# Six input tiles by column halves in place of four: the two gate tiles of the first block join them

## The chip, the cores and the metric

One core of one Trainium2 chip runs the whole program. The metric is device time in microseconds, the median of several executions, in float32 throughout.

## The reference, cut to what matters

Two blocks of two layers each act on 1024 tokens of width 1024 (the first block carries 256 context tokens beside them). Only the first block is touched here. Each of its layers normalizes and modulates the tokens, multiplies by `w_in` (2592 columns), mixes in three branches (a gated depthwise convolution, windowed attention, a gated linear recurrence), and multiplies by `w_out`. The convolution branch:

```python
hl = _rms_norm(xl) * (1.0 + scale[:, None]) + shift[:, None]
pl = _project(hl, w_in)          # a_val, a_glu, a_gate (256 columns each), b_q, b_k, ...

def _conv_branch(p, conv_w, conv_b, ln_w, ln_b):
    u = p['a_val'] * jax.nn.sigmoid(p['a_glu'])
    u = lax.conv_general_dilated(
        u, conv_w[:, None, :].astype(u.dtype), window_strides=(1,),
        padding=((CONV_KERNEL // 2, CONV_KERNEL // 2),),      # CONV_KERNEL = 31
        dimension_numbers=('NWC', 'WIO', 'NWC'), feature_group_count=CONV_WIDTH) + conv_b
    uf = u.astype(F32)
    mu = jnp.mean(uf, axis=-1, keepdims=True)
    var = jnp.mean(jnp.square(uf - mu), axis=-1, keepdims=True)
    u = ((uf - mu) * lax.rsqrt(var + NORM_EPS) * ln_w + ln_b).astype(p['a_val'].dtype)
    return jax.nn.silu(u) * jax.nn.silu(p['a_gate'])
```

The first layer computes the context tokens' branches too, the second only those that the other tokens need.

## The kernel before, in words

Activations lie transposed, channels on the partitions and tokens along the free dimension: 1280 columns in layer 0 (1024 tokens and 256 of context), 1024 in layer 1 for this branch. One *tile* of a projection is 128 output channels: a weight matrix of 1024 x 128, read as eight pieces of 128 x 128. To hold float32 accuracy every operand is split into a rounded part and a remainder (`hi`, `lo`), and each piece takes three matmuls (lines 562 to 564, or 590 to 592: weights hi by h hi, hi by lo, lo by hi). So 512 columns of a tile are 24 matmuls of 128x512.

`stream()` writes the order of all tiles by hand into `SEQ`. SyncE loads the weights in that order into two buffers of `raw` (L434), GpSimd splits them (`split_weights`, L2117 and L2118) once TensorE is through with the tile that used the buffer before (two tiles back in the stream), and TensorE multiplies. The first `SKEW1` tiles of a layer of the first block (glu0, val0, glu1, val1; then come gate0, gate1, bk, bv, q0 ...) are run by column halves: first all of them on columns 0 to 511 (pass 0), then all of them on the rest (pass 1: 512 + 256 columns in layer 0, 512 in layer 1). Their weights are loaded and split once for each pass. The other tiles take all their columns at once. glu0 is run piece by piece as h comes (`project_as_ready`, `row_tile`), with the waits for its accumulators ahead of its first piece.

Each chunk of up to 512 columns takes an accumulator bank, three in turn (`psum_of`: q % 3, `acc_free0` to `acc_free2`), and TensorE may start a chunk only when the one three before it has been read out:

- ScalarE (`sigmoids`, L1115) reads glu0 and glu1 and writes their sigmoid. glu1's waits until VectorE has used up glu0's (`u_ready`).
- VectorE (`gated`, L1657) reads val0 and val1 and multiplies by the sigmoid into `cv_u`.
- ScalarE (L1136) reads gate0 and gate1 and writes their Silu into `x`.

In between, both engines make h for pass 1: VectorE scales a tile (`scaled`, L1582), ScalarE rounds it (`round_h`, L1080), VectorE takes the remainder (`split_h`, L1595), eight times. VectorE's order is four tiles of h, val0's product, four tiles of h, val1's product, then pass 1's products, and then the convolution (L1673 and L1675, 31 taps for each of two channel tiles, `conv_ready` after each). In layer 0 TensorE computes 16 pieces of modulation (L598) after gate1. In both layers it then multiplies bk and waits for the convolution, to average it (L654) and its squares (L659). Behind that come ScalarE's square root by Ln and Exp, its Silu (L1156), VectorE's product with the gate (L1696), and only then may ScalarE read out bk (L1104) and the attention begin.

SyncE stores layer 0's output `x` to DRAM before layer 1 (L498, `store0`), and ScalarE waits for that before it writes a gate into `x`.

Of the kernel before, what the change touches and what calls it, by code (L numbers as in the profile page):

```python
# [16 lines left out]
ACT = mybir.ActivationFunctionType  # L17
# [34 lines left out]

PASS_ALL = [CH_ALL[:1], CH_ALL[1:]]
PASS_LAT = [CH_LAT[:1], CH_LAT[1:]]
SKEW1, SKEW2, SKEWF = 4, 8, 4

ORDER2 = [range(8), (0, 1, 4, 5, 2, 3, 6, 7)]

# [1 line left out]
def stream():  # L60

    seq = []
    for l in range(2):
        every = lambda n: PASS_ALL if l == 0 or n in KV1 else PASS_LAT
        for p in range(2):
            for i, n in enumerate(IN1[:SKEW1]):
                seq.append(("in1", l, i, 8, every(n)[p], p))
        for i, n in list(enumerate(IN1))[SKEW1:]:
            seq.append(("in1", l, i, 8, sum(every(n), []), 0))
        for p in range(2):  # L70
            for d in range(DT):
                seq.append(("out1", l, d, 8, (PASS_ALL if l == 0 else PASS_LAT)[p], p))
    for l in range(2):
        for p in range(2):
            for i in ORDER2[p]:
                seq.append(("in2", l, i, 8, PASS_LAT[p], p))
        for i in range(SKEW2, len(IN2)):
            seq.append(("in2", l, i, 8, CH_LAT, 0))
        for p in range(2):
            for d in range(DT):  # L80
                seq.append(("out2", l, d, 8, PASS_LAT[p], p))
        for p in range(2):
            for i in range(SKEWF):
                seq.append(("up", l, i, 8, PASS_LAT[p], p))
        for f in range(NF):
            if f >= SKEWF // 2:
                seq.append(("up", l, 2 * f, 8, CH_LAT, 0))
                seq.append(("up", l, 2 * f + 1, 8, CH_LAT, 0))
            if f in AFTER:
                g = AFTER[f]  # L90
                last = g == len(GROUPS) - 1
                for p in range(2 if last else 1):
                    for d in range(DT):
                        seq.append(("down", l, (g, d), GROUPS[g][1] - GROUPS[g][0], PASS_LAT[p] if last else CH_LAT, p))
    return seq


SEQ = stream()
INDEX = {e[:3] + e[5:]: g for g, e in enumerate(SEQ)}
FIRST_CHUNK = np.cumsum([0] + [len(e[4]) for e in SEQ]).tolist()  # L100
# [76 lines left out]
def two_mixers(nc, xT, cT, w_mod, w_in1, w_out1, vec1, vec2, vec3, sinks, gla_up,  # L177
# [27 lines left out]
    x = x_[:, :].rearrange("p (j t) -> p j t", t=T)  # L205
# [42 lines left out]
    def norm_buffers(n, p):  # L248

        if n < 2:  # L250
            v = [nt[:, i * W1:(i + 1) * W1] for i in range(5)]
            return v[0], v[1], v[2], v[3:5]
        v = [nt[:, i * W2:(i + 1) * W2] for i in range(7)]
        return v[2 * p], v[2 * p + 1], v[4], v[5:7]
# [93 lines left out]
    sem = {n: nc.alloc_semaphore(n) for n in names}  # L348
# [3 lines left out]
    def columns(n, p):  # L352

        return (0, 512) if p == 0 else (512, 768 if n < 2 else 512)
# [48 lines left out]
    def proj_index(l, name, p=0):  # L403
        return INDEX[("in1", l, IN1.index(name), p)]

    def in2_index(l, name, p=0):
        return INDEX[("in2", l, IN2.index(name), p)]
# [6 lines left out]
    def psum_of(q):  # L414
        return psum[q % 3]


    with block:
        @block.sync
        def _(sp):  # L420
            loaded = [0]

            def load_weights(g):
                kind, l, i, nk, _, _ = SEQ[g]
                if g >= 2:
                    sp.wait_ge(sem["w_split"], g - 1)
                src = {"in1": w_in1, "out1": w_out1, "in2": w_in2, "out2": w_out2, "up": w_ffn}.get(kind)
                if kind == "down":
                    grp, d = i
                    f0, f1 = GROUPS[grp]  # L430
                    src = w_down[l, d, :, f0 * P:f1 * P]
                else:
                    src = src[l, i]
                sp.dma_start(raw[:, (g % 2) * 1024:(g % 2) * 1024 + nk * P], src)\  # L434
                  .then_inc(sem[f"raw_in{g % 2}"], 16)
# [108 lines left out]
        def _(pe):  # L544
# [3 lines left out]
            def row_tile(g, kt, hi, lo, ready, before):  # L548

                _, _, _, nk, chunks, _ = SEQ[g]  # L550
                wh, wl = w_hi[:, (g % 2) * 1024:], w_lo[:, (g % 2) * 1024:]
                if kt == 0:
                    pe.wait_ge(sem["w_split"], g + 1)
                    for ci in range(len(chunks)):
                        q = FIRST_CHUNK[g] + ci
                        if q >= 3:
                            pe.wait_ge(sem[f"acc_free{q % 3}"], q // 3)
                ws = slice(kt * P, (kt + 1) * P)
                pe.wait_ge(sem[ready], before + kt + 1)
                for ci, (t0, n) in enumerate(chunks):  # L560
                    o = psum_of(FIRST_CHUNK[g] + ci)[:, 0:n]
                    mm(o, wh[:, ws], hi[:, kt, t0:t0 + n], start=kt == 0, stop=False)  # L562
                    mm(o, wh[:, ws], lo[:, kt, t0:t0 + n], start=False, stop=False)
                    last = mm(o, wl[:, ws], hi[:, kt, t0:t0 + n], start=False, stop=kt == nk - 1)  # L564
                    if kt == nk - 1:
                        last.then_inc(sem["acc_ready"], 1)
# [465 lines left out]
        def _(act):  # L1032
            A = nc.scalar.activation
            steps = [0]

            def link(ins):

                steps[0] += 1
                ins.then_inc(sem["act_step"], 1)
                act.wait_ge(sem["act_step"], steps[0])  # L1040
# [29 lines left out]
            def round_h(n, p, j):  # L1070

                _, _, _, ts = norm_buffers(n, p)
                t0, w = columns(n, p)
                act.wait_ge(sem[f"t_ready{p}"], 8 * n + j + 1)
                if n >= 2:
                    A(h2_hi[:, j, t0:t0 + w], ts[j % 2][:, 0:w], ACT.Copy).then_inc(sem["hhi_ready"], 1)
                    return
                for c0, cw, r in [(t0, 512, 0), (S, C, 1)][:1 + p]:
                    c = 48 * n + 2 * j + r
                    last = A(h_hi[:, j, c0:c0 + cw], ts[j % 2][:, c0 - t0:c0 - t0 + cw], ACT.Identity, bias=mod[:, c:c + 1])  # L1080
                last.then_inc(sem["hhi_ready"], 1)
# [14 lines left out]
            for l in layers:  # L1096
# [10 lines left out]
                def sigmoids(j, p):  # L1107

                    if j:
                        act.wait_ge(sem["u_ready"], 4 * l + 1 + 2 * p)  # L1110
                    g = proj_index(l, f"glu{j}", p)
                    for ci, (t0, w) in enumerate(SEQ[g][4]):
                        q = FIRST_CHUNK[g] + ci
                        act.wait_ge(sem["acc_ready"], q + 1)
                        link(A(cv_sig[:, t0:t0 + w], psum_of(q)[:, 0:w], ACT.Sigmoid))  # L1115
                        act.sem_inc(sem[f"acc_free{q % 3}"], 1)
                        act.sem_inc(sem["glu_ready"], 1)
# [6 lines left out]
                sigmoids(1, 0)  # L1124
                for j in range(4, DT):
                    round_h(l, 1, j)
                sigmoids(0, 1)
                sigmoids(1, 1)
                if l:
                    act.wait_ge(sem["store0"], 16)  # L1130
                for j in range(2):
                    g = proj_index(l, f"gate{j}")
                    for ci, (t0, w) in enumerate(SEQ[g][4]):
                        q = FIRST_CHUNK[g] + ci
                        act.wait_ge(sem["acc_ready"], q + 1)
                        link(A(x[:, j, t0:t0 + w], psum_of(q)[:, 0:w], ACT.Silu))  # L1136
                        act.sem_inc(sem[f"acc_free{q % 3}"], 1)
                act.sem_inc(sem["gate_ready"], 1)
                for a in range(len(LATE_MOD) if l == 0 else 0):
                    act.wait_ge(sem["wm_used"], 4 + a + 1)  # L1140
# [66 lines left out]
                for j in range(4):  # L1207
                    if j or l:
                        act.wait_ge(sem["rope_ready"], 5 * l + 1 + j)
                    g = proj_index(l, f"q{j}")  # L1210
# [112 lines left out]
            def evacuate2(g, dst, func, scale=1.0):  # L1323
                for ci, (t0, w) in enumerate(SEQ[g][4]):
                    q = FIRST_CHUNK[g] + ci
                    act.wait_ge(sem["acc_ready"], q + 1)
                    link(A(dst[:, t0:t0 + w], psum_of(q)[:, 0:w], func, scale=scale))  # L1327
                    act.sem_inc(sem[f"acc_free{q % 3}"], 1)

            for l in layers:  # L1330
# [6 lines left out]
                def gates(j, p):  # L1337
                    act.wait_ge(sem[f"store{1 + l}_{p}"], 16)
                    evacuate2(in2_index(l, f"su{j}", p), x2[:, j], ACT.Gelu_apprx_tanh)
# [955 lines left out]
```

## Time and profile before

| | before |
|---|---|
| median of 3 runs | 4418.41 us (4415.34 to 4421.36) |
| the profiled execution, its time | 4409.52 us |
| its span, first to last instruction | 4407.7 us |
| mean granted TensorE clock | 0.956 |
| TensorE matmuls busy | 3960.8 us, 90% |
| VectorE busy | 2155.2 us, 49% |
| ScalarE busy | 1098.7 us, 25% |
| GpSimd busy | 1393.9 us, 32% |

The busy times are averages over stages with different limits. The two stretches that the change touches are the beginning of layer 0 (some 76 to 300 us) and of layer 1 (some 1013 to 1200 us). A matmul's start is exact, its end is modelled, so the length of a run of matmuls is read from start to start.

### The profile page before, as it was taken

How to read it: one execution, taken by the hardware profiler on the slowest of the kernel's cores; microseconds unless marked ns; L12 is line 12 of the kernel's file. 1: busy time of each engine (PE TensorE's matmuls, PEld its weight loads, DVE VectorE, ACT ScalarE, POOL GpSimd, SP SyncE). 2: the span in 40 equal slices, each digit the busy share in tenths (PEclk: the TensorE clock that was granted, in tenths of full speed). 3: DMA queues.
4: the chain of work that ended last, by engine and by line, in shares of the span. 5: the costliest groups of instructions: out<-in, count | busy, mean ns of one | idle time of the engine just before them, and what ended most of it. 6: DMA issues, size and time to landing. Idle time of an engine off the chain costs nothing.

```text
span 4407.7 us, 47585 instructions
## 1 busy us (share of the span) xinstructions
PE 3960.8 (90%) x18476; PEld 3120.2 (71%) x18476; DVE 2155.2 (49%) x2838; ACT 1098.7 (25%) x2057; POOL 1393.9 (32%) x924
## 2 busy tenths in 40 slices
PE   5979999799399997889989999998889899999997
PEld 2657778677267776667767888886677677888885
DVE  3755650846656445642336445444442246444545
ACT  3114552122145422322222111111213222111112
POOL 1121001344110123552335333333543254333333
PEclk9989999999699998999989999999899899999998
DMA  4310000033000001420122111111310031111112
GB/s 171 136 70 20 11 1 26 20 102 119 10 20 11 21 6 63 146 69 29 34 79 84 48 48 39 48 46 50 115 53 29 24 116 55 53 51 48 43 50 70
DMA packets 83952, 245.97 MB, mean 56 GB/s; under 512 B 8720, under 2 KB 15888, under 8 KB 82960
## 3 DMA queue, kind: packets, MB, share of 16 engines
q1 hardware_dynamic: 83728, 242.93, 16.6%
q8 instruction: 147, 2.41, 0.2%
q14 instruction: 77, 0.63, 0.0%
HBM read 226.12 MB, written 16.78 MB: 55 GB/s over the span
## 4 chain that ended last, share of the span: by engine, by line
PE 73%; DVE 19%; ACT 4%; issue 2%; DMA 1%; POOL 1%; DVEq 0%; SPq 0%; ACTq 0%; POOLq 0%
PE bank L590 19%; PE bank L591 19%; PE bank L592 19%; DVE wk L1675 4%; PE bank L712 2%; DVE nt L1582 1%; PE bank L698 1%; DVE gw L1810 1%; DVE gw L1799 1%; PE bank L689 1%; PE bank L687 1%; DVE wk L1732 1%; DVE nt L1571 1%; PE bank L562 1%; PE bank L564 1%
## 5 line engine op out<-in xcount | busy, mean ns | idle before, releaser
L590 PE MATMUL bank<-h_hi,w_hi 128*128 128x512 f32 (+1 forms) x3504 | 1381.9, 394 | 43.2 <-POOLq L2119 26.2
L591 PE MATMUL bank<-h_lo,w_hi 128*128 128x512 f32 (+1 forms) x3504 | 1359.7, 388 | 0.0
L592 PE MATMUL bank<-h_hi,w_lo 128*128 128x512 f32 (+1 forms) x3504 | 1358.9, 388 | 0.0
L2117 POOL CAST w_hi<-raw 128x1024 fp32r<-128x1024 f32 (+2 forms) x386 | 389.7, 1010 | 2239.2 <-PE bank L592 1718.5
L2118 POOL TENSOR_TENSOR w_lo<-raw,w_hi 128x1024 fp32r<-128x1024 f32 (+2 forms) x386 | 839.4, 2175 | 30.9
L590 PEld LDWEIGHTS bank<-h_hi,w_hi 128*128 128x128 f32 x3504 | 667.0, 190 | 202.2 <-POOLq L2119 30.9
L591 PEld LDWEIGHTS bank<-h_lo,w_hi 128*128 128x128 f32 x3504 | 666.4, 190 | 151.2 <-issue 10.0
L592 PEld LDWEIGHTS bank<-h_hi,w_lo 128*128 128x128 f32 x3504 | 665.6, 190 | 144.5
L590 PE MATMUL bank<-g_hi,w_hi 128*128 128x512 f32 x704 | 282.2, 401 | 39.6 <-DVEq L2082 26.6
L1327 ACT ACTIVATE wk<-bank 128x512 f32<-128x512 f32 x200 | 119.1, 596 | 791.4 <-PE bank L592 770.4
L2067 DVE TENSOR_SCALAR wk<-wk,v 128x1024 f32<-128x1024 f32 x88 | 89.0, 1011 | 456.5 <-ACTq L1519 438.3
L591 PE MATMUL bank<-g_lo,w_hi 128*128 128x512 f32 x704 | 280.1, 398 | 0.0
L592 PE MATMUL bank<-g_hi,w_lo 128*128 128x512 f32 x704 | 280.0, 398 | 0.0
L2055 DVE TENSOR_TENSOR x<-bank,x 128x512 f32<-128x512 f32 x192 | 132.6, 691 | 205.6 <-PE bank L592 201.2
L1675 DVE SCALAR_TENSOR_TENSOR wk<-wk,v 128x1024 f32<-128x1024 f32 (+1 forms) x180 | 191.1, 1090 | 4.3
L2069 DVE SCALAR_TENSOR_TENSOR wk<-wk,v 128x1024 f32<-128x1024 f32 x88 | 190.3, 2163 | 5.3
L2140 POOL TENSOR_TENSOR wk<-wk,x 128x1024 f32<-128x1024 f32 x10 | 23.5, 2347 | 533.8 <-ACTq L1214 404.7
L590 PEld LDWEIGHTS bank<-g_hi,w_hi 128*128 128x128 f32 x704 | 133.9, 190 | 76.8 <-DVEq L2082 27.5
L1055 ACT ACTIVATE nt<-x 128x512 f32<-128x512 f32 (+1 forms) x128 | 83.9, 658 | 405.6 <-DVE nt L1571 316.9
L712 PE MATMUL bank<-wk 128*128 128x128 f32 x1280 | 166.5, 276 | 0.0
L1521 ACT ACTIVATE wk<-wk 128x1024 f32<-128x1024 f32 x44 | 46.7, 1061 | 452.8 <-DVEq L2074 452.8
L592 PEld LDWEIGHTS bank<-g_hi,w_lo 128*128 128x128 f32 x704 | 134.1, 190 | 31.6
(247 smaller groups left out, 4797.7 us busy)
## 6 DMA issues: line engine op xcount, KB each, us to landing
raw<-w_in SPq DMA_DIRECT2D x114, 512.0 KB, 3.5
raw<-w_ffn SPq DMA_DIRECT2D x96, 512.0 KB, 3.5
raw<-w_out SPq DMA_DIRECT2D x64, 512.0 KB, 3.7
x<-w_mod SPq DMA_DIRECT2D x16, 1024.0 KB, 4.8
raw<-w_down SPq DMA_DIRECT2D x64, 256.0 KB, 2.6
wk<-residual SPq DMA_DIRECT2D x48, 256.0 KB, 2.6
raw<-w_down SPq DMA_DIRECT2D x48, 192.0 KB, 2.3
gw<-w_mod SPq DMA_DIRECT2D x4, 2048.0 KB, 21.2
```

The costliest lines, as they stand in the source:

```text
L590: mm(o, wh[:, ws], hi[:, at_, t0:t0 + n], start=kt == 0, stop=False)
L591: mm(o, wh[:, ws], lo[:, at_, t0:t0 + n], start=False, stop=False)
L592: last = mm(o, wl[:, ws], hi[:, at_, t0:t0 + n], start=False, stop=kt == nk - 1)
L712: last = mm(out_bank(i)[:, 0:P], at_vz[:, kt, g, :], at_pt[i % 2][:, c * P:(c + 1) * P], start=g == 0 and c == 0, stop=g == 1 and c == len ...
L1055: A((sq if d else acc)[:, 0:w], src[:, d, t0:t0 + w], ACT.Square).then_inc(sem[f"sq_ready{p}"], 1)
L1327: link(A(dst[:, t0:t0 + w], psum_of(q)[:, 0:w], func, scale=scale))
L1675: ins = V.scalar_tensor_tensor(dst, src, vl("conv_w", 31 * j + i), dst, ALU.mult, ALU.add)
L2055: link(V.tensor_tensor(x2[:, d, t0:t0 + w], psum_of(q)[:, 0:w], x2[:, d, t0:t0 + w], ALU.add))
L2067: link(V.tensor_scalar(c, u[:, 2:], w2("conv_w", 88 + wi), w2("conv_b", wi), ALU.mult, ALU.add))
L2069: link(V.scalar_tensor_tensor(c, u[:, 1:S + 1], w2("conv_w", 44 + wi), c, ALU.mult, ALU.add))
L2117: link(G.tensor_copy(w_hi[:, sl], raw[:, sl]))
L2118: link(G.tensor_tensor(w_lo[:, sl], raw[:, sl], w_hi[:, sl].bitcast(F32), ALU.subtract))
```

## The change

`SKEW1` goes from 4 to 6, so gate0 and gate1 are also run by column halves, and each of them is loaded and split twice in a layer. On ScalarE the Silu of the gates is taken apart by pass: that of pass 0 stands behind the rounding of h and ahead of pass 1's sigmoids, that of pass 1 behind them. The wait for the store moves ahead with it. VectorE's program is the same.

```diff
-SKEW1, SKEW2, SKEWF = 4, 8, 4
+SKEW1, SKEW2, SKEWF = 6, 8, 4
...
                 for j in range(4, DT):
                     round_h(l, 1, j)
+                def gates(p):
+
+                    for j in range(2):
+                        g = proj_index(l, f"gate{j}", p)
+                        for ci, (t0, w) in enumerate(SEQ[g][4]):
+                            q = FIRST_CHUNK[g] + ci
+                            act.wait_ge(sem["acc_ready"], q + 1)
+                            link(A(x[:, j, t0:t0 + w], psum_of(q)[:, 0:w], ACT.Silu))
+                            act.sem_inc(sem[f"acc_free{q % 3}"], 1)
+
+                if l:
+                    act.wait_ge(sem["store0"], 16)
+                gates(0)
                 sigmoids(0, 1)
                 sigmoids(1, 1)
-                if l:
-                    act.wait_ge(sem["store0"], 16)
-                for j in range(2):
-                    g = proj_index(l, f"gate{j}")
-                    for ci, (t0, w) in enumerate(SEQ[g][4]):
-                        q = FIRST_CHUNK[g] + ci
-                        act.wait_ge(sem["acc_ready"], q + 1)
-                        link(A(x[:, j, t0:t0 + w], psum_of(q)[:, 0:w], ACT.Silu))
-                        act.sem_inc(sem[f"acc_free{q % 3}"], 1)
+                gates(1)
                 act.sem_inc(sem["gate_ready"], 1)
```

TensorE's rows where layer 0's val1 (pass 0, bank 0) ends, before the change: the next rows are glu0's second pass, its chunks in banks 1 and 2, with the semaphores that the row waits for.

```order
L591 MATMUL bank0<-h_lo_63,w_hi_50 128x512
L592 MATMUL bank0<-h_hi_62,w_lo_51 128x512
L562 MATMUL bank1<-h_hi_62,w_hi_50 128x512 [waits acc_free2,h_ready,acc_free1,w_split]
L563 MATMUL bank1<-h_lo_63,w_hi_50 128x512
L564 MATMUL bank1<-h_hi_62,w_lo_51 128x512
L562 MATMUL bank2<-h_hi_62,w_hi_50 128x256
```

The same place after the change, where gate0 (bank 1) and gate1 (bank 2) stand between, 48 matmuls in all, and glu0's second pass comes behind them:

```order
L592 MATMUL bank0<-h_hi_62,w_lo_51 128x512
L590 MATMUL bank1<-h_hi_62,w_hi_50 128x512 [waits acc_free1,w_split]
...
L590 MATMUL bank2<-h_hi_62,w_hi_50 128x512 [waits acc_free2,w_split]
...
L592 MATMUL bank2<-h_hi_62,w_lo_51 128x512
L562 MATMUL bank0<-h_hi_62,w_hi_50 128x512 [waits acc_free1,h_ready,acc_free0,w_split]
```

What stood there waited for banks 1 and 2 together with its first piece. Now gate0 waits for bank 1 alone, and glu0's second pass waits for banks 0 and 1, that is for val1 of pass 0 and gate0 of pass 0 to be read out.

ScalarE's rows behind the last rounding of h in layer 0, before:

```order
L1080 ACTIVATE h_hi_62<-nt_60,mod_57 128x256
L1115 ACTIVATE wk1_66<-bank1 128x512 [waits acc_ready]
L1115 ACTIVATE wk1_66<-bank2 128x256 [waits act_step,acc_ready]
L1115 ACTIVATE wk1_66<-bank2 128x512 [waits act_step,acc_ready,u_ready]
L1115 ACTIVATE wk1_66<-bank0 128x256 [waits act_step,acc_ready]
L1136 ACT_TABLE_LOAD [waits act_step]
```

And after (the Silu of the gates is line 1134 there):

```order
L1080 ACTIVATE h_hi_62<-nt_60,mod_57 128x256
L1134 ACT_TABLE_LOAD
L1134 ACTIVATE x_61<-bank1 128x512 [waits acc_ready]
L1134 ACTIVATE x_61<-bank2 128x512 [waits act_step,acc_ready]
L1115 ACT_TABLE_LOAD [waits act_step]
L1115 ACTIVATE wk1_66<-bank0 128x512 [waits acc_ready]
```

The two gate chunks of pass 0 have moved ahead of the four sigmoids of pass 1, with a table load on either side, and the sigmoids read other banks.

## Rows read from the trace of the kernel before

**Rows 1.** The page: busy time of each engine, and the chain by engine and line.

```profile
PE 3960.8 (90%) x18476; PEld 3120.2 (71%) x18476; DVE 2155.2 (49%) x2838; ACT 1098.7 (25%) x2057; POOL 1393.9 (32%) x924
...
PE 73%; DVE 19%; ACT 4%; issue 2%; DMA 1%; POOL 1%; DVEq 0%; SPq 0%; ACTq 0%; POOLq 0%
PE bank L590 19%; PE bank L591 19%; PE bank L592 19%; DVE wk L1675 4%; PE bank L712 2%; DVE nt L1582 1%; PE bank L698 1%; DVE gw L1810 1%; DVE gw L1799 1%; PE bank L689 1%; PE bank L687 1%; DVE wk L1732 1%; DVE nt L1571 1%; PE bank L562 1%; PE bank L564 1%
```

**Rows 2.** TensorE's waits, whole run: us in total, times, longest.

```profile
PE bank L654 <- DVEq L1677: 54.2, 3, 36.8
...
PE bank L562 <- ACTq L1116: 6.1, 1, 6.1
```

**Rows 3.** Timeline of TensorE, layer 0: start us, us, engine, line, tiles.

```profile
107.19 0.39 PE L592 MATMUL bank<-h_hi,w_lo 128*128 128x512 f32 x1
113.65 0.77 PE L562 MATMUL bank<-h_hi,w_hi 128*128 128x512 f32 x1 [6.08 <-ACTq L1116]
...
123.76 0.39 PE L590 MATMUL bank<-h_hi,w_hi 128*128 128x512 f32 x1
...
149.08 0.40 PE L590 MATMUL bank<-h_hi,w_hi 128*128 128x512 f32 x1
...
177.05 0.28 PE L592 MATMUL bank<-h_hi,w_lo 128*128 128x256 f32 x1
```

**Rows 4.** Timeline of VectorE, and TensorE behind it: the convolution in layer 0.

```profile
150.03 3.35 DVE L1673 TENSOR_SCALAR wk<-wk,v 128x1024 f32<-128x1024 f32 x2 [0.24 <-DVE wk L1657]
...
206.20 57.09 DVE L1675 SCALAR_TENSOR_TENSOR wk<-wk,v 128x1024 f32<-128x1024 f32 x60
...
263.41 4.11 PE L654 MATMUL bank<-wk,cst 128*128 128x512 f32 x6 [4.57 <-DVEq L1677]
```

**Rows 5.** Timeline of TensorE, layer 1.

```profile
1043.69 0.40 PE L562 MATMUL bank<-h_hi,w_hi 128*128 128x512 f32 x1
...
1048.94 0.50 PE L562 MATMUL bank<-h_hi,w_hi 128*128 128x512 f32 x1 [1.61 <-DVE h_lo L1595]
...
1053.33 0.40 PE L590 MATMUL bank<-h_hi,w_hi 128*128 128x512 f32 x1
...
1069.84 0.40 PE L592 MATMUL bank<-h_hi,w_lo 128*128 128x512 f32 x1
...
1159.97 3.78 PE L654 MATMUL bank<-wk,cst 128*128 128x512 f32 x4 [36.81 <-DVEq L1677]
```

**Rows 6.** Timeline of VectorE and ScalarE, layer 0: reading out, the last rounding, a table load.

```profile
111.89 0.68 DVE L1657 TENSOR_TENSOR wk<-bank,wk 128x512 f32<-128x512 f32 x1
...
122.19 0.69 DVE L1657 TENSOR_TENSOR wk<-bank,wk 128x512 f32<-128x512 f32 x1
...
112.76 0.60 ACT L1115 ACTIVATE wk<-bank 128x512 f32<-128x512 f32 x1 [4.61 <-DVEq L1659]
...
119.97 1.12 ACT L1080 ACTIVATE h_hi<-nt,mod 128x512 fp32r<-128x512 f32 x2 [1.19 <-DVE nt L1582]
...
141.38 1.28 ACT L1136 ACT_TABLE_LOAD   x1 [0.17 <-ACT wk L1115]
```

**Rows 7.** Windows (from:to, length, busy of each engine, granted clock, DMA), behind the pause.

```profile
113.70:116.90 3.20, 3.20 (x9) 2.72 (x10) 2.97 (x6) 2.18 (x4) 0.00 (x0) 0.50 0.25 92
```

**Rows 8.** Timeline of GpSimd and VectorE, layer 1, the last tiles of h.

```profile
1045.50 2.44 POOL L2118 TENSOR_TENSOR w_lo<-raw,w_hi 128x1024 fp32r<-128x1024 f32 x1
...
1053.64 1.04 POOL L2117 CAST w_hi<-raw 128x1024 fp32r<-128x1024 f32 x1 [5.69 <-PE bank L564]
...
1045.62 3.26 DVE L1595 SCALAR_TENSOR_TENSOR h_lo<-nt,mod,h_hi 128x512 fp32r<-128x512 f32 x2
...
1050.05 1.14 DVE L1595 SCALAR_TENSOR_TENSOR h_lo<-nt,mod,h_hi 128x512 fp32r<-128x512 f32 x2
...
1052.39 0.69 DVE L1657 TENSOR_TENSOR wk<-bank,wk 128x512 f32<-128x512 f32 x1
```

**Rows 9.** Timeline of SyncE's queue, the store of x.

```profile
1012.02 0.58 SPq L498 DMA_DIRECT2D residual<-x  x1
```

**Rows 10.** The page: DMA issues, count, KB each, us to landing.

```profile
residual<-x SPq DMA_DIRECT2D x1, 4096.0 KB, 12.5
```

## The prediction

> **What bounds the kernel now.** I read four views. The page comes first: TensorE is busy for 90% of the span and carries 73% of the chain, but the fourth entry of the chain by line is no matmul, it is VectorE's line 1675, the depthwise convolution, with 4% [rows 1]. Next I asked whom TensorE waits for. Its longest entry over the whole run is the wait of L654, the matmuls that average the convolution's output, for VectorE: 54.2 us in three waits, the longest 36.8 [rows 2]. So around the convolution the matmul stream isn't the bound. VectorE is, and what counts there is when the convolution can start.
>
> It starts when VectorE has made the last gated tile of u, from the second half of val1. In layer 0, TensorE ends val1's second pass at 149.08 [rows 3] and VectorE starts the convolution at 150.03. It ends at 206.20 + 57.09 = 263.29, and L654 follows at 263.41 after 4.57 us of idle TensorE [rows 4]. In layer 1 TensorE is through with val1 at 1069.84 + 0.23 = 1070.07, and when the convolution's second half lets L654 go at 1159.97, TensorE has sat idle 36.81 us [rows 5]. In both layers TensorE already waits for the convolution, so each microsecond by which the convolution starts later comes out at L654, with no slack in between. Behind L654 stands a chain of mean, variance, Silu, product and bk's evacuation, over four engines, and nothing there runs on a clock of its own.
>
> The second thing to read is what the change aims at, TensorE's pause between the two passes. In layer 0 val1's first pass ends at 107.4 and glu0's second pass starts at 113.65, with 6.08 us idle for ScalarE's L1116 [rows 3]. That is no wait for h. Line 1116 gives back an accumulator. There are three accumulators in turn, and the waiting chunks need bank 1, which VectorE frees with val0's product (end 111.89 + 0.68 = 112.57), and bank 2, which ScalarE frees with glu1's sigmoid (end 112.76 + 0.60 = 113.36) [rows 6].
>
> **The change, part by part.** The matmuls are the same in number and shape. Two tiles per layer are loaded and split twice: four loads of 512 KB and four splits more.
>
> *Layer 0.* gate0's first pass takes the place behind val1. It uses bank 1, so it starts 0.29 us (as 113.36 to 113.65 now) after 112.57, at 112.86: the pause shrinks by 0.8 us and isn't filled. Price of a tile: three tiles of 512 columns take 1070.07 - 1053.33 = 16.74, 5.58 each [rows 5]; three of 512 + 256 columns take 149.08 - 123.76 = 25.32, 8.44 each. glu0's second pass takes 123.76 - 113.65 = 10.11, which is 1.67 more than 8.44, since TensorE comes out of the pause at half its clock (granted 0.50 in the pause's wake, the level of 1.2 GHz) [rows 3, 7]. That 1.67 now falls on gate0. So gate0 ends at 112.86 + 5.58 + 1.67 = 120.1 and gate1 at 125.7. glu0's second pass needs bank 0, which VectorE frees with val1's product (122.19 + 0.69 = 122.88 [rows 6], and some 2 us later if the split released by gate0's end at 120.1 gets in its way), and bank 1, freed by gate0's Silu on ScalarE: behind the last rounding of h (119.97 + 1.12 = 121.1), a table load of 1.28 and 0.60 us of work, near 123.0 [rows 6]. Both lie before 125.7: no new pause. Four tiles of 8.44 end at 159.5, against 149.08: **the convolution starts 10.4 us later**. The two gate tiles of 5.58 cost 11.16, and 0.8 of it comes back.
>
> *Layer 1.* TensorE enters glu0's second pass straight behind val1, at 1043.69, and needs until 1053.33, 9.64 us for 5.58 of work, since it waits for tiles of h (1.61 us is the first and longest of three such waits) [rows 5]. Here the gates do fill something. They end at 1043.69 + 11.16 = 1054.85, when all of h should be there, and glu0 then takes 5.58: without anything else, 1060.4 against 1053.33, 7.1 us later. Against that stands GpSimd. The split released by the tile just ended comes now at 1053.64, behind VectorE's work on h; with the change gate0 ends at 1049.25, so the split falls on VectorE's last pieces of h. What this costs shows just before: with the split's subtraction (2.44 us from 1045.50) beside it, VectorE's pair of L1595 takes 3.26 us, and undisturbed the next such pair takes 1.14: 2.1 us [rows 8]. Between 2.1 and the 2.9 that it would be with a second, short piece caught I take 2.6: val1's product ends not at 1052.39 + 0.69 = 1053.08 but near 1055.7. glu0 needs the bank that it frees, and starts 0.3 later, at 1056.0, in place of 1054.85: 1.15 us lost (0 if the split slips past VectorE, 2.5 if it hits two pieces). val1 ends at 1056.0 + 4 x 5.58 = 1078.3 against 1070.07: **8.2 us later**, between 7.1 and 9.6.
>
> *Costed at nothing.* The extra loads sit under tiles of 5.58 us, which a split of 1.04 + 2.44 = 3.5 us [rows 8] already fits behind. Two table loads more per layer on ScalarE (1.28 each [rows 6]) lie between waits for TensorE of 5 us and more; without that cover each would cost its 1.28, once. ScalarE's wait for the store of x now stands ahead of layer 1's second sigmoids: the store is issued at 1012.02 [rows 9] and its 4096 KB land in 12.5 us [rows 10], near 1025, long before the first passes end at 1043.69. The convolution itself keeps its company: one split at its start in layer 0 (its first pair takes 3.35 us [rows 4]) and three in layer 1, in both kernels. The late modulation loads follow gate1's load, some 10 us later than now, and are first used at 177 [rows 3].
>
> A tile of 5.58 us over 24 matmuls makes 232 ns from one matmul to the next at 512 columns [rows 5]. The Trainium skill (TensorE: Matmul & The Clock Gate, section "Wait — 56ns, not 53.3ns?") gives 215.7 ns for that at the full clock; by its figure, as an estimate, the two gates would take 10.35 us in place of 11.16, and the sum would be about 17 us. The trace doesn't agree with it here, so the row decides.
>
> **Sum.** 10.4 + 8.2 = 18.6 us, nothing given back later. The profiled execution took 4409.5 us, 1.8 more than its span of 4407.7; with the change it would take 4428. The median of the runs shown, 4418.4, lies 8.9 above the profiled one, so I add the same 18.6 to it: **4437**, 0.42% more. 0.2% (8.8 us) is about what a measurement of this kernel can tell from no change.
>
> **Rivals.**
> *A, the matmul stream decides.* If the convolution's start had slack, only TensorE's own progress would count. In layer 0 it would be through with both gates at 159.5 + 2 x 8.44 = 176.4 against 177.2 now [rows 3], in layer 1 at 1078.3 + 11.16 = 1089.5 against 1070.07 + 4 x 5.58 = 1092.4. That saves 0.8 + 2.9 = 3.7 us: 4415, not slower. It decides only if L654 didn't wait for VectorE; the waits of 4.57 and 36.81 us speak against it.
> *B, new waits.* The gates' accumulators are freed late, on ScalarE behind rounding and table load or on VectorE behind two splits. In layer 0 bank 0 has 2.8 us of slack; if two splits of 2.9 us fall on VectorE's last tiles, TensorE pauses 3 us, starts again at half clock (1.67), and layer 1 does likewise (2.5 + 1.67 in place of 1.15). That adds 7.7: 4445.
> *C, one layer counts.* If the loss in layer 0 were taken up behind L654, by work that now waits for something else, 8.2 us remain: 4427. I see no such work, only waits chained to each other.
>
> **How the numbers follow.** Forecast 0.78, A 0.07, B 0.08, C 0.07. The forecast's own range is 16.5 us (no collision in layer 1, so 7.1, and 1 us of slack found in layer 0) to 20 (the worst collision in layer 1, 9.6), with 3 us on either side, as far as the runs shown lie from their median: 4432 to 4441. Reaching to C and B gives 4426 to 4445. Slower by over 0.2% holds the forecast, B and half of C, 0.89; within 0.2% half of C and most of A, 0.09; faster 0.02.
>
> **What would show it.** In the profile after: L1673's first row near 160.4 in layer 0 and near 1079.5 in layer 1 (plus layer 0's delay, so near 1090); L654's wait in layer 0 grown from 4.6 to about 15.8, in layer 1 its first (54.2 - 4.6 - 36.8 = 12.8) to about 24 with the second unchanged, 76 in all; a pause of some 5.3 us before gate0's first matmul, not gone; glu0's second pass without waits inside, 8.4 and 5.6 us; VectorE's pieces of h in layer 1 beside a split. The forecast is wrong if L654 does not move with the convolution's start, or if val1's second pass ends earlier than 159 because TensorE's pause was filled after all.

## The result, and the profile after

| | before | after |
|---|---|---|
| median of 5 runs | 4418.41 us (4415.09 to 4421.36) | 4437.76 us (4435.75 to 4438.7) |
| the profiled execution, its time | 4409.52 us | 4435.75 us |
| its span | 4407.7 us | 4434.0 us |
| mean granted TensorE clock | 0.956 | 0.951 |

The changed kernel takes 1.0046 times as long (95% interval 1.0035 to 1.0058), 19.35 us more by the medians. 4437 was predicted. The two profiled executions lie further apart, 26.2 us, because that of before is 8.9 us below its own median and that of after only 2.0. So stages are compared below from an anchor at their beginning, not by absolute times: in layer 0 the first piece of h of pass 1 on VectorE (93.43 us before, 94.39 after, so 0.96 is taken off), in layer 1 the issue of the store ([rows 9] and 1025.02 after, so 13.00 is taken off). In the lines of after, VectorE's and GpSimd's line numbers are 5 higher, and the Silu of the gates is L1134.

First the page of after (busy time of each engine, the chain by engine):

```profile
PE 3964.2 (89%) x18476; PEld 3122.5 (70%) x18476; DVE 2160.4 (49%) x2838; ACT 1104.9 (25%) x2061; POOL 1410.1 (32%) x932
...
PE 74%; DVE 18%; ACT 3%; issue 2%; DMA 1%; POOL 1%; SPq 0%; DVEq 0%; ACTq 0%; POOLq 0%
```

It shows next to nothing beside [rows 1]: as many matmuls, 3.4 us more of them, eight GpSimd instructions more. The loss isn't work, so it has to be in the waits. TensorE's waits over the whole run (us in total, times, longest):

```profile
PE bank L654 <- DVEq L1682: 76.3, 3, 36.8
...
PE bank L590 <- DVEq L1663: 5.2, 1, 5.2
```

The wait for the convolution has grown from 54.2 to 76.3 us, with the same longest one [rows 2]. And the 6.1 us in which glu0's second pass waited for ScalarE are now 5.2 in which gate0 waits for VectorE's product: the pause has changed its owner and is still there. TensorE's timeline in layer 0:

```profile
113.75 0.76 PE L590 MATMUL bank<-h_hi,w_hi 128*128 128x512 f32 x1 [5.19 <-DVEq L1663]
...
118.58 0.63 PE L592 MATMUL bank<-h_hi,w_lo 128*128 128x512 f32 x1
119.00 0.53 PE L590 MATMUL bank<-h_hi,w_hi 128*128 128x512 f32 x1
119.36 0.39 PE L591 MATMUL bank<-h_lo,w_hi 128*128 128x512 f32 x1
...
127.50 0.40 PE L562 MATMUL bank<-h_hi,w_hi 128*128 128x512 f32 x1
...
161.26 0.40 PE L590 MATMUL bank<-h_hi,w_hi 128*128 128x512 f32 x1
...
257.48 2.31 PE L654 MATMUL bank<-wk,cst 128*128 128x512 f32 x6
...
275.51 4.48 PE L654 MATMUL bank<-wk,cst 128*128 128x512 f32 x6 [15.72 <-DVEq L1682]
```

gate0 starts 5.6 us after the start of the last matmul before it (108.16), of which 5.19 are idle. Both gates take 127.50 - 113.75 = 13.75 us, the four tiles behind them 161.26 - 127.50 = 33.76, which is 4 x 8.44. val1's second pass ends at 161.26, against 149.08 [rows 3]. The last two rows are the reading that matters. Before, TensorE reached L654 at this moment:

```profile
256.52 2.31 PE L654 MATMUL bank<-wk,cst 128*128 128x512 f32 x6
```

That is 0.96 us earlier, exactly the anchor's difference. By the time it needs the convolution, TensorE is where it was before; it then waits 15.72 us in place of 4.57. VectorE's timeline in layer 0 and in layer 1:

```profile
112.87 0.68 DVE L1662 TENSOR_TENSOR wk<-bank,wk 128x512 f32<-128x512 f32 x1
...
162.21 3.35 DVE L1678 TENSOR_SCALAR wk<-wk,v 128x1024 f32<-128x1024 f32 x2 [0.24 <-DVE wk L1662]
...
218.38 57.02 DVE L1680 SCALAR_TENSOR_TENSOR wk<-wk,v 128x1024 f32<-128x1024 f32 x60
...
1063.83 4.34 DVE L1600 SCALAR_TENSOR_TENSOR h_lo<-nt,mod,h_hi 128x512 fp32r<-128x512 f32 x4
1068.10 0.68 DVE L1662 TENSOR_TENSOR wk<-bank,wk 128x512 f32<-128x512 f32 x1
...
1092.61 0.81 DVE L1678 TENSOR_SCALAR wk<-wk,v 128x1024 f32<-128x1024 f32 x1 [0.24 <-DVE wk L1662]
```

The convolution starts at 162.21 in layer 0, against 150.03 [rows 4]: less the anchor's 0.96, **11.2 us later**. Its first half takes the same time, 218.38 - 162.21 = 56.17 us, as 206.20 - 150.03 did. In layer 1 it starts at 1092.61; before, at 1071.28:

```profile
1071.28 0.81 DVE L1673 TENSOR_SCALAR wk<-wk,v 128x1024 f32<-128x1024 f32 x1 [0.24 <-DVE wk L1657]
```

So 67.59 us behind the store's issue in place of 59.26: **8.3 us later**. The two make 19.5 us, the medians' difference being 19.35. That agreement is closer than the evidence: the kernel before was profiled once, and 59.26 is low for it. Two other kernels of the experiments below, profiled once each, have layer 1 exactly as before (gates by halves in layer 0 alone; accumulators read out early in layer 0 of the kernel before), and there the convolution starts 60.63 and 60.59 us behind the store. The first of them:

```profile
1084.88 0.81 DVE L1683 TENSOR_SCALAR wk<-wk,v 128x1024 f32<-128x1024 f32 x1 [0.24 <-DVE wk L1667]
```

with the store issued at 1024.25. The difference is TensorE's clock. Behind the waits for h inside glu0's second pass the matmuls of these two come 0.43 us apart (granted clock 0.65 from 1063.20 to 1067.00 in the first), while in the profiled execution of before they come 0.23 apart (granted 1.00 from 1051.00 to 1053.30). Against 60.6 layer 1's delay is **7.0 us**, and the changed kernel, whose TensorE has no such waits there, starts at 67.5 to 67.6 in all three of its versions that keep this part (67.59, 67.64, 67.51). So layer 1 costs 7.0 to 8.3 us and the two layers 18.2 to 19.5. In layer 0 the start of the convolution in the kernel before is steady: 56.60, 56.60 and 56.49 us behind the anchor in three kernels that leave it alone.

GpSimd in layer 1, beside the four pieces of h at 1063.83:

```profile
1062.28 1.36 POOL L2122 CAST w_hi<-raw 128x1024 fp32r<-128x1024 f32 x1 [1.74 <-PE bank L592]
1063.71 2.46 POOL L2123 TENSOR_TENSOR w_lo<-raw,w_hi 128x1024 fp32r<-128x1024 f32 x1
```

Two undisturbed pairs would take 2 x 1.14 us [rows 8]; with the split's subtraction beside them the four take 4.34, 2.1 us more.

### The profile page after: what moved, and what is told of

It reads as the page before. It is cut to its first block, busy times and chain, and to the rows that moved or that the text cites. A ratio compares the mean times of both kernels' runs of the same rounds, so it can differ in the third digit from the quotient of the medians.

```text
span 4434.0 us, 47613 instructions
## 1 busy us (share of the span) xinstructions
PE 3964.2 (89%) x18476; PEld 3122.5 (70%) x18476; DVE 2160.4 (49%) x2838; ACT 1104.9 (25%) x2061; POOL 1410.1 (32%) x932
## 4 chain that ended last, share of the span: by engine, by line
PE 74%; DVE 18%; ACT 3%; issue 2%; DMA 1%; POOL 1%; SPq 0%; DVEq 0%; ACTq 0%; POOLq 0%
PE bank L590 19%; PE bank L591 19%; PE bank L592 19%; DVE wk L1680 4%; PE bank L712 2%; PE bank L698 1%; DVE nt L1587 1%; PE bank L689 1%; DVE gw L1815 1%; DVE gw L1804 1%; PE bank L687 1%; DVE nt L1576 1%; DVE wk L1737 1%; PE bank L562 1%; DVE h_lo L1603 1%
## 5 line engine op out<-in xcount | busy, mean ns | idle before, releaser
L2123 POOL TENSOR_TENSOR w_lo<-raw,w_hi 128x1024 fp32r<-128x1024 f32 (+2 forms) x390 | 848.7, 2176 | 31.2
L591 PEld LDWEIGHTS bank<-h_lo,w_hi 128*128 128x128 f32 x3504 | 666.3, 190 | 151.7 <-issue 10.1
```

Source lines behind the costliest of these rows:

```text
L591: mm(o, wh[:, ws], lo[:, at_, t0:t0 + n], start=False, stop=False)
L2123: link(G.tensor_tensor(w_lo[:, sl], raw[:, sl], w_hi[:, sl].bitcast(F32), ALU.subtract))
```

## Experiments

Each kernel was run in five rounds beside the kernel before; ratios are to that, with 95% intervals. Of the eight, four ask where the loss comes from (which layer, which mechanism, one gate or two), and four ask what the convolution's start and the pause are worth by themselves. The ratio is not the quotient of the medians, so the two give differences that are up to 2.4 us apart; both are given where it matters.

### One layer at a time

`SKEW1` becomes a pair, one number for each layer; where it is 4, ScalarE reads the gates behind the second sigmoids as before.

```diff
-SKEW1, SKEW2, SKEWF = 6, 8, 4
+SKEW1, SKEW2, SKEWF = (6, 4), 8, 4
...
-            for i, n in enumerate(IN1[:SKEW1]):
+            for i, n in enumerate(IN1[:SKEW1[l]]):
...
```

Layer 0 alone, (6, 4). Expected:

> Gates by column halves in layer 0 only. My theory (what counts is when val1's second half is done and the convolution can start): the convolution of layer 0 starts some 11 us later than before, as in the profile of the changed kernel, and layer 1 is untouched, so 10 to 12 us slower. The rival (the extra loads, splits and table loads cost the time, whose half is here): about 9.7 us, too near to tell apart by the time alone; by it the convolution's start would not account for the loss.

Measured: 4430.25 us against 4416.26, ratio 1.0029 (1.0017 to 1.004): 12.8 us by the ratio, 14.0 by the medians. The convolution starts at 161.76 us with the anchor at 93.93, which is 67.83 against 56.60 before: 11.2 later. TensorE waits 65.6 us at L654 in all.

Layer 1 alone, (4, 6). Expected:

> Gates by column halves in layer 1 only. My theory: 8.2 us slower (7 to 10), all of it a later start of layer 1's convolution; layer 0's first wait of L654 stays at 4.6 us. With the layer 0 kernel the sum should give the whole loss of 19.4 us.

Measured: 4423.91 us against 4416.26, ratio 1.0015 (1.0006 to 1.0024): 6.6 us by the ratio, 7.7 by the medians. Layer 0's convolution stays at 149.92 (anchor 93.32, so 56.60 as before); in layer 1 VectorE's timeline has

```profile
1079.83 0.81 DVE L1683 TENSOR_SCALAR wk<-wk,v 128x1024 f32<-128x1024 f32 x1 [0.24 <-DVE wk L1667]
```

with the store issued at 1012.19: 67.64 us, 8.4 later than in the profile of before and 7.0 later than the 60.6 of the other two kernels with that layer 1. L654 waits 65.4 us.

By the ratios the two make 12.8 + 6.6 = 19.4 us, by the medians 14.0 + 7.7 = 21.7; with intervals of some 4 to 5 us on either side of each, the times alone only say that both layers cost something. The traces say how much: 11.2 and 7.0 to 8.4 later. The waits add up too: 54.2 + 11.4 + 11.2 = 76.8 against 76.3. (L654's wait in layer 1 grows by 10.9, more than the convolution's delay, since TensorE reaches it 2.7 us earlier than before: 1140.55 - 23.76 is 91.77 us behind the store, 1119.38 - 12.85 was 94.51. Rival A had worked out 2.9.) Each layer pays for itself, which rules out rival C.

### The same halves, behind val1

This is the kernel before, with both gates run by halves too and the same four loads and splits more, but both halves of both behind val1's second pass. ScalarE reads them behind the second sigmoids, as before. What it tells apart: the place of the gates from the halving itself.

```diff
-        for i, n in list(enumerate(IN1))[SKEW1:]:
+        for p in range(2):
+            for i, n in list(enumerate(IN1))[SKEW1:6]:
+                seq.append(("in1", l, i, 8, every(n)[p], p))
+        for i, n in list(enumerate(IN1))[6:]:
...
-                for j in range(2):
-                    g = proj_index(l, f"gate{j}")
+                for j, p in ((0, 0), (1, 0), (0, 1), (1, 1)):
+                    g = proj_index(l, f"gate{j}", p)
...
```

Expected:

> The same extra loads, splits and chunks, but both passes of the gates stand behind val1's second pass. My theory: the convolution starts when it did before, so no change (within 2 us). The rival (loads, splits, more weight traffic beside VectorE cost the time): near 19 us slower.

Measured: 4426.4 us, ratio 1.0024 (1.0015 to 1.0034), about 10.1 us slower. Neither number. In layer 0 the convolution starts where it did, 149.97 us with the anchor at 93.48, as expected; in layer 1 it starts 60.81 us behind the store, near the 60.6 of the two kernels with that layer unchanged. But it lasts longer. VectorE's timeline:

```profile
149.97 3.35 DVE L1677 TENSOR_SCALAR wk<-wk,v 128x1024 f32<-128x1024 f32 x2 [0.24 <-DVE wk L1661]
153.36 57.08 DVE L1679 SCALAR_TENSOR_TENSOR wk<-wk,v 128x1024 f32<-128x1024 f32 x60
...
211.76 57.00 DVE L1679 SCALAR_TENSOR_TENSOR wk<-wk,v 128x1024 f32<-128x1024 f32 x60
...
1080.18 52.43 DVE L1679 SCALAR_TENSOR_TENSOR wk<-wk,v 128x1024 f32<-128x1024 f32 x30
```

The first half takes 211.76 - 149.97 = 61.79 us in place of 56.17, and in layer 1 the first thirty taps take 52.43 in place of 47.13. GpSimd's timeline in layer 0, beside it:

```profile
149.33 1.04 POOL L2121 CAST w_hi<-raw 128x1024 fp32r<-128x1024 f32 x1 [4.94 <-PE bank L595]
150.45 2.72 POOL L2122 TENSOR_TENSOR w_lo<-raw,w_hi 128x1024 fp32r<-128x1024 f32 x1
154.91 1.04 POOL L2121 CAST w_hi<-raw 128x1024 fp32r<-128x1024 f32 x1 [1.74 <-PE bank L595]
156.03 3.25 POOL L2122 TENSOR_TENSOR w_lo<-raw,w_hi 128x1024 fp32r<-128x1024 f32 x1
160.49 1.29 POOL L2121 CAST w_hi<-raw 128x1024 fp32r<-128x1024 f32 x1 [1.21 <-PE bank L595]
```

Three splits stand beside the first half in place of one (in layer 1 five in place of three). The stretch lies where they lie: while the subtraction at 156.03 ran, VectorE had two instructions in 3.25 us, and the longest of L1679's 180 took 3.31 us, their median being 1.29. The weight loads that run then too are not what does it. In layer 1 of the kernel before the first thirty taps, with three splits beside them and hardly a transfer (DMA share 0.00 and 0.02 beside two of the subtractions), take 47.13 us and the second thirty, with no split, 39.59. And in layer 0, with no split but a DMA share of 0.67 (180 to 200 us), VectorE gets through 25 instructions in 20 us, as against 19 in 15.7 without transfers. Two splits more cost VectorE 5.6 us in layer 0 and 5.3 in layer 1, some 2.7 each and 10.9 in all; TensorE's wait at L654 grows by just that, from 54.2 to 65.1. So this run shows a price that I had set at nothing, and which could have been taken for half of the change's loss had only the total been read. It is no part of it: in the changed kernel the convolution's first halves take 56.17 and, from 1092.61 to the second half's first row at 1140.59, 47.98 us (48.13 before). What follows for the change is that without the gates' new place TensorE's extra loads and halves alone don't move the convolution's start, and the new place does, by 11.2 and by 7.0 to 8.3.

### One gate alone

`SKEW1` is (5, 5): gate0 joins, gate1 stays. If the loss were proportional, this would cost half. Expected:

> Only gate0 joins (five tiles by halves). If the loss went by TensorE's work put ahead, one tile of 5.58 us per layer would cost half of 19.4, near 10 us. My theory says that it costs nearly as much as two: glu0's second pass then waits for the accumulator that VectorE frees with val1's product (in layer 0 near 123 to 125 in place of 120.1, in layer 1 near 1055.7 where the split released by gate0 collides), so +8 to +10 in layer 0 and +8 in layer 1, 16 to 18 us in all.

Measured: 4431.02 us, ratio 1.0034 (1.0021 to 1.0046), 14.8 us by the medians. In layer 0 the expectation held and the price of one gate is that of two: the convolution starts at 163.39 with the anchor at 93.88, 12.9 us later. TensorE's timeline has two pauses:

```profile
113.23 0.76 PE L590 MATMUL bank<-h_hi,w_hi 128*128 128x512 f32 x1 [5.19 <-DVEq L1668]
...
126.28 0.77 PE L562 MATMUL bank<-h_hi,w_hi 128*128 128x512 f32 x1 [5.18 <-DVEq L1668]
```

Behind gate0 alone, glu0's second pass waits for val1's bank, whose product VectorE reaches only at 125.29, behind h with a split beside it, and it comes out of that at half clock again. In layer 1 the expectation failed: the convolution is only 2.8 us later (62.10 behind the store in place of 59.26), or 1.5 against 60.6. With one gate between, glu0's first chunk falls on the bank that glu1's sigmoid frees early, in both layers. In layer 1 that is its only chunk, so it starts at 1063.51 with h still coming and fills the wait as before. In layer 0 the second pass has a second chunk (256 columns), which falls on val1's bank, and the program waits for both banks ahead of the first piece. With three banks in turn, the number of chunks between two tiles and the number that the later one needs decide whose read-out it waits for; I had reasoned with val1's bank for both layers.

### The convolution's start, moved the other way

If the start decides, moving it earlier must pay. On both kernels, VectorE starts the first channel tile's taps right behind val0's second product; val1's second product comes 8 taps later in layer 0, 6 in layer 1.

```diff
                 gated(0, 1)
-                gated(1, 1)
                 for j in range(2):
                     for i in range(CK):
+                        if j == 0 and i == (8, 6)[l]:
+                            gated(1, 1)
...
```

On the kernel before, expected:

> The kernel before (four tiles by halves), but VectorE starts the first half of the convolution as soon as its own input is whole (behind val0's second product) and takes val1's second product in between, behind 8 taps in layer 0 and 6 in layer 1. My theory: faster. Layer 1 gains the 10 us that VectorE sat idle between the two products, layer 0 only until TensorE's bk is the bound, its 4.6 us of wait and some 1.8 of half clock behind it: 14 to 17 us faster in all, L654's waits in layer 0 gone. The rival (the convolution's start is not what sets the time): no change.

Measured: **4405.04 us against 4418.06, ratio 0.9972 (0.9962 to 0.9983)**. This version beats both kernels. VectorE's timeline, from the convolution's first row to the product that waits for its mean:

```profile
133.39 3.35 DVE L1674 TENSOR_SCALAR wk<-wk,v 128x1024 f32<-128x1024 f32 x2 [0.24 <-DVE wk L1657]
...
196.74 57.01 DVE L1676 SCALAR_TENSOR_TENSOR wk<-wk,v 128x1024 f32<-128x1024 f32 x60
...
261.68 3.26 DVE L1686 TENSOR_TENSOR wk<-wk,bank 128x512 f32<-128x512 f32 x6 [7.15 <-PE bank L654]
```

Measured from the anchor (93.66 here), the convolution starts 16.9 us earlier but ends only 9.8 earlier (253.75 - 93.66 = 160.1 against 263.29 - 93.43 = 169.9 [rows 4]): two splits more stand beside it, and val1's products lie inside it. Of those 9.8 us, L1686 gets 6.1 (261.68 against 267.55 in the profile of before), since TensorE arrives at L654 at 257.18 without any wait: there its own stream decides now. In layer 1 the start moves from 59.26 to 49.36 us behind the store, and the end from 147.84 to 143.12, by 4.7. The two make 10.8 of the 12.4 (ratio) to 13.0 (medians) measured. Most of the rest is the low baseline again: in the two kernels with layer 1 unchanged the convolution ends 149.2 us behind the store, and TensorE's clock fell here too (granted 0.60 from 1045 to 1049). Against 149.2 layer 1 gains 6.1, and the sum is 12.2.

On the changed kernel, expected:

> The same edit on the changed kernel (six tiles by halves). My theory: in layer 0 the convolution now has slack beside TensorE's bk, so the later start costs 0 to 2 us there and no longer 11; in layer 1 it still costs 8. So 8 to 10 us slower than the same edit on the kernel before, some 6 us faster than the kernel before itself. The rival (the change costs its 19.4 us whatever sets the time): 19 slower than its partner, so 3 slower than before.

Measured: 4419.16 us, ratio 1.0008 (0.9999 to 1.0016), 14.1 us above the four-tile version, midway between the 8 to 10 expected and the rival's 19. The total doesn't choose between them; the trace says where the time lies. TensorE's timeline in layer 0:

```profile
256.73 2.31 PE L654 MATMUL bank<-wk,cst 128*128 128x512 f32 x6
264.81 3.81 PE L654 MATMUL bank<-wk,cst 128*128 128x512 f32 x6 [5.77 <-DVEq L1683]
```

The start is 10.7 us later than in the four-tile version (144.12 against 133.39), and 7.0 of it come out at L1691 (268.66 against 261.68); the rest went into the time that VectorE had to spare there in the four-tile version. In layer 1 it is 7.1 (56.49 against 49.36 behind the store). 7.0 + 7.1 = 14.1, the whole difference. I had put layer 0 at 0 to 2. What I left out are the two splits beside the convolution, although the run of the halves behind val1 had just shown their price: it ends at 207.48 + 57.22 = 264.70, and 5.6 us earlier, at 259.1, it would have been there when TensorE is through with L654's first half (256.73 + 2.31 = 259.04). So where VectorE has slack, part of the delay is hidden, and that is the condition that rival A named; but here it hides a third of it, in one layer.

### The pause by itself

In layer 0, VectorE makes val0's product behind two tiles of h in place of four and val1's behind six in place of eight; on the changed kernel ScalarE also reads gate0 ahead of its last two roundings.

```diff
-                tiles(l, 1, range(4))
-                gated(0, 0)
-                tiles(l, 1, range(4, DT))
-                gated(1, 0)
+                if l == 0:
+                    tiles(l, 1, range(2))
+                    gated(0, 0)
+                    tiles(l, 1, range(2, 6))
+                    gated(1, 0)
+                    tiles(l, 1, range(6, DT))
...
```

On the changed kernel, expected:

> The changed kernel with its accumulators read out earlier in layer 0: VectorE takes val0's product behind two tiles of h in place of four and val1's behind six in place of eight, ScalarE writes gate0's Silu ahead of the last two roundings. My theory (TensorE's pause between the passes is a wait for banks, and the loss is the later convolution): the pause of 5.2 us and the half clock behind it go, the gates run in it, and layer 0's convolution starts some 3 to 4 us later than before in place of 11. So 11 to 13 us slower than before in place of 19. The rival (the pause is a wait for h or for weights): no different from the changed kernel.

Measured: 4434.42 us against 4416.38, ratio 1.0039 (1.0027 to 1.0052); 11 to 13 us slower was expected and 17 to 18 came. The interval overlaps that of the change itself, so the total doesn't show a gain. TensorE's timeline:

```profile
120.09 0.40 PE L592 MATMUL bank<-h_hi,w_lo 128*128 128x512 f32 x1
123.21 0.48 PE L562 MATMUL bank<-h_hi,w_hi 128*128 128x512 f32 x1 [2.71 <-DVEq L1668]
123.52 0.60 PE L563 MATMUL bank<-h_lo,w_hi 128*128 128x512 f32 x1
123.91 0.63 PE L564 MATMUL bank<-h_hi,w_lo 128*128 128x512 f32 x1
```

The pause ahead of gate0 is gone: TensorE runs from val1 through both gates without a wait, which shows that it was a wait for a bank and nothing else. But the gates are through earlier, and the splits that their ends release fall on VectorE while it makes h; val1's product comes at 122.37, TensorE pauses 2.71 us in another place and its clock falls to half right behind that (granted 0.50 from 123.90 to 126.00). The convolution starts 64.46 us behind the anchor (159.52 - 95.06), 7.9 later than before: 3.4 better than the change in the layer's own trace, where 7 to 8 was hoped for.

On the kernel before, expected:

> VectorE's same order (layer 0, products behind two and six tiles of h) on the kernel before. glu0's second pass can start near 110 and runs as tiles of h come; it ends when the last tile does, near 123.5, where it ends now. My theory: no change, within 2 us, since filling the pause with work that must wait for h brings nothing to the convolution's start. If the pause itself cost the time, some 5 us faster.

Measured: 4417.22 us against 4416.38, ratio 1.0000 (0.9991 to 1.0009), as expected. The pause shrinks from 6.1 to 1.7 us, and glu0 then waits for pieces of h instead (1.06, 1.00 and 3.08 us). In layer 0 the convolution starts 152.43 - 94.39 = 58.04 us behind the anchor, 1.4 later than before and not at the same moment, as was expected: behind the last of these waits TensorE is at half clock for a while (granted 0.62 from 124 to 126), which is most of the 1.4. So TensorE's pause in the kernel before is worth nothing, within the 4 us that the times resolve, because h isn't there yet.

## Why the prediction was right

**What decides** is the convolution's start on VectorE, with no slack behind it. Shown: L654's wait went from 54.2 to 76.3 us (76 predicted), in layer 0 to 15.72 (15.8), in layer 1 its first to 76.3 - 15.72 - 36.8 = 23.8 (24), and the second stayed at 36.8. The runs that moved the start by 7 us and more moved the time with it, in both directions, and in full except where VectorE had slack (a third of it, in one layer). The halves behind val1 left the start and moved the end, and the time went with the end. The two shifts that are smaller, 3.4 us earlier than in the changed kernel and 1.4 later than before, are below what the times resolve.

**Layer 0, 10.4 us predicted, 11.2 measured.** Gate0's start held: 113.75 less the anchor's 0.96 is 112.79, for 112.86. The four tiles of 8.44 held to the hundredth, without a new pause, and so did bank 0 (val1's product came in time). The term that was mis-sized is the half clock behind the pause. I took 1.67 us from the kernel before [rows 3, 7], where it stands behind a pause of 6.1 us; the two gates took 13.75 us where 11.16 is their work, so behind one of 5.2 us it cost 2.59. The 0.9 us between is the whole error of this layer's start. 0.3 us more came out behind it: VectorE's product that needs L654 is 11.5 us later (280.03 against 267.55, less 0.96).

**Layer 1, 8.2 predicted, 8.3 measured, and part of that is luck.** The collision came as forecast: four pieces of h took 4.34 us, val1's product ended at 1068.78, that is 1055.8 less 13.0 (1055.7 predicted), glu0 started 0.2 us behind it (1068.94), and val1 was through 22.5 us later. All that is the changed kernel's side, and it held. The other side, where before lets val1 end, came from one profiled execution in which the clock did not fall behind the waits for h. Against the two that kept layer 1 as it was, the delay is 7.0, and 8.2 is 1.2 too much.

**Costed at nothing:** the four loads and splits, table loads, the store's wait, the convolution's company. The sum bears it out in the changed kernel. But "two splits more per layer are free" is true only of where they fall here. Behind val1 they cost 10.9 us, and my text gave no number for the case that this cover is gone.

**Sum and the median.** 18.6 predicted, 19.35 measured, with an interval of 15.5 to 25.6 by the ratio. The errors of the two layers, 0.8 too little and 0 to 1.2 too much, have opposite signs; that the sum comes out within 1 us is more than its terms can promise. Adding the sum to the median, and not to the profiled execution, was the right choice: the profiled pair alone would have said 26.2. Where its other 6.7 us lie I can only name in part: 1.0 ahead of the first anchor, 0.3 behind L654 in layer 0, and 1.8 at one row of L659 in layer 1 (3.78 us against 1.98, TensorE at half its clock in the one and not in the other); the rest is spread over stretches that the change doesn't touch.

**The rivals.** A (TensorE's stream decides) needed a TensorE that doesn't wait at L654. It came there at the same moment in layer 0, where A had it 0.8 us earlier (the longer half clock ate that), and 2.7 us earlier in layer 1, and then waited in both. B's second pause didn't occur in the changed kernel, but it is real: it appears with one gate, 5.18 us. C is ruled out by the two runs of one layer.

## What to carry to other kernels

Before putting work into a pause of a busy engine, ask who waits longest for whom in the same stage: here TensorE's pause of 6 us was worth nothing (taking 4.4 us of it away changed nothing that the times show), while 11.2 us of independent tiles put ahead of the tile that starts VectorE's 100 us cost their full length in layer 0 and 7.0 to 8.3 us in layer 1, where they stand in for waits for h. What feeds the long chain goes first, and filler goes behind it; where the chain's first step can start on half its input, start it (12 to 13 us here). A helper's work released by a tile's end moves with the tile, so look up on whose instructions it falls after the change.

## What the runs showed of the hardware

A split on GpSimd is a cast and a subtraction of 128x1024. With VectorE idle (from 1059.88 to 1070.35 in the kernel before) they take 1.04 and 2.40 us:

```profile
1060.34 2.40 POOL L2118 TENSOR_TENSOR w_lo<-raw,w_hi 128x1024 fp32r<-128x1024 f32 x1
```

Beside VectorE's `scalar_tensor_tensor` with two inputs from SBUF a split cost VectorE 2.5 to 2.8 us (two more in the run of the halves behind val1, 5.6 and 5.3; three in layer 1 of the kernel before, 47.13 - 39.59), and GpSimd's own subtraction took between 2.46 and 3.26. So most of the split's 3.44 us are lost to VectorE. One instruction of VectorE took 3.31 us in the run of the halves behind val1 (median 1.29), about as long as the subtraction beside it; that the two engines took turns is what this looks like, and no run separates it from both running slower. The Trainium skill (SBUF — State Buffer, section "Who interferes with whom") says that a VectorE instruction with two SBUF inputs contends with a GpSimd instruction that reads SBUF; these rows agree, and give its price.

How long TensorE stays at half clock behind a pause went with the pause here. Counted from the first matmul behind it to the first at full pace, it is 3.5, 3.5, 3.3 and 3.5 us behind the 6.1 us pause of the four kernels that keep it (before, layer 1 alone, the halves behind val1, the convolution early on four tiles), and 5.6, 5.6, 4.7, 4.7 and 5.2 us behind the five pauses of 5.2 us (after, layer 0 alone, the convolution early on six tiles, and both pauses of the one-gate kernel). The last of these has glu0's pieces behind it, as before has, so the work behind isn't what makes the difference. Why the shorter pause is followed by the longer half clock no run shows. The windows of after (from:to, length, busy of each engine with counts, granted clock, DMA):

```profile
113.70:119.00 5.30, 5.25 (x12) 4.13 (x13) 4.91 (x9) 3.16 (x6) 0.00 (x0) 0.50 0.36 104
119.10:127.40 8.30, 8.30 (x37) 6.78 (x36) 5.28 (x9) 3.65 (x6) 3.98 (x2) 0.99 0.02 2
```

Half clock, 1.2 GHz, in the first, and full clock, 2.4 GHz, in the second. In layer 1 TensorE kept its full clock through the waits for h in the profiled execution of before and fell to half in the two kernels whose layer 1 is the same, which is 1.3 to 1.4 us at the convolution's start. So a term that rests on the clock of one profiled execution carries about 1 us of doubt.
